# Loading the experts' second matrix with two neighbouring rows per partition

## The reference

```
hdn   = x @ w_mlp1[e] + b_mlp1[e]                      # w_mlp1[e]: 1024 x 2048
x_glu = min(hdn[:, ::2], 7)
x_lin = clip(hdn[:, 1::2], -7, 7)
act   = x_glu * sigmoid(1.702 * x_glu) * (x_lin + 1)   # tokens x 1024
y     = act @ w_mlp2[e] + b_mlp2[e]                    # w_mlp2[e]: 1024 x 1024
```

## Time and profile before

| | |
|---|---|
| median of 3 runs | 1247.48 us |
| the profiled execution | 1247.71 us |
| its span, first to last instruction | 1245.9 us |
| TensorE busy (share of the span) | 1166.1 us (94%) |
| VectorE / ScalarE busy | 407.1 / 225.8 us |
| DMA, mean over the span | 365 GB/s, 454.95 MB |
| mean granted TensorE clock | 0.997 of full speed |

### The profile page before, as it was taken

The page is one execution under the profiler, slowest core; times in us unless marked ns, Lnnn a source line. Parts: engine busy times, 40 slices in busy tenths (PEclk is TensorE's granted clock), DMA queues, the critical chain, the costliest instruction groups (busy, mean ns, idle before and its releaser), DMA issues.

```text
span 1245.9 us, 13489 instructions
## 1 busy us (share of the span) xinstructions
PE 1166.1 (94%) x5408; PEld 531.5 (43%) x5408; DVE 407.1 (33%) x674; ACT 225.8 (18%) x344; POOL 8.7 (1%) x17
## 2 busy tenths in 40 slices
PE   8999999999999999999999999899999998999997
PEld 5887777876333333333233333233333332333232
DVE  4765656764322222322222222222222222222221
ACT  3544546442001000100011000000000000000001
POOL 0100000000000000000000000000000000000000
PEclk9999999999999999999999999999999999999999
DMA  9654443689999999999999999999999999999996
GB/s 356 235 176 161 144 152 124 191 324 417 386 417 417 418 417 417 418 416 418 417 417 418 417 417 417 417 417 417 417 417 417 418 417 417 417 417 417 416 417 263
DMA packets 95908, 454.95 MB, mean 365 GB/s; under 512 B 7376, under 2 KB 7408, under 8 KB 62896
## 3 DMA queue, kind: packets, MB, share of 16 engines
q1 hardware_dynamic: 94112, 449.34, 89.7%
q10 hardware_dynamic: 960, 2.44, 0.6%
q0 software_dynamic: 784, 2.38, 0.6%
HBM read 453.09 MB, written 1.05 MB: 365 GB/s over the span
## 4 chain that ended last, share of the span: by engine, by line
PE 50%; DMA 41%; SPq 3%; DVE 3%; ACT 2%; issue 2%; ACTq 0%; DVEq 0%
PE PS L1404 13%; DMA raw<-in_w_mlp 13%; DMA merge_raw<-in_w_mlp 9%; DMA hi_raw<-in_w_mlp 9%; PE PS L1410 8%; PE PS L1234 5%; PE PS L1232 5%; PE PS L1233 4%; PE PS L1440 4%; DMA gate_raw<-in_w_mlp 4%; DMA prob_raw<-in_w_mlp 2%; DMA mT<-in_w_mlp 2%; DMA low_raw<-in_w_mlp 2%; SPq L495 2%; PE PS L1382 1%
## 5 line engine op out<-in xcount | busy, mean ns | idle before, releaser
L1404 PE MATMUL PS<-merge_raw,XG 128*64 128x512 f32 x640 | 145.9, 597 | 8.2 <-DMA merge_raw<-in_w_mlp 8.0
L1142 DVE TENSOR_SCALAR hT<-PS 128x512 f32<-128x512 f32 x32 | 22.1, 692 | 379.0 <-PE PS L1404 379.0
L759 ACT ACTIVATE hT<-hT 128x512 f32<-128x512 f32 x31 | 19.5, 631 | 567.1 <-DVE hT L1142 567.1
L1404 PE MATMUL PS<-raw,XG 128*64 128x512 f32 x464 | 106.4, 597 | 6.7 <-DMA raw<-in_w_mlp 6.4
L826 DVE TENSOR_TENSOR rest<-raw,mix_hi 128x2048 fp32r<-128x2048 f32 x38 | 87.0, 2292 | 53.4 <-ACT mix_hi L615 53.3
L1070 DVE COPY XG<-PS 128x512 f32<-128x512 f32 x32 | 22.1, 691 | 239.9 <-PE PS L1389 239.9
L1232 PE MATMUL PS<-mix_hi,hTh 128*128 128x512 f32 x224 | 89.8, 401 | 3.2 <-DVE hTl L998 1.6
L1077 DVE TENSOR_TENSOR X<-X,PS 128x512 f32<-128x512 f32 x120 | 74.4, 682 | 51.9 <-PE PS L1440 51.9
L1234 PE MATMUL PS<-mix_hi,hTl 128*128 128x512 f32 x224 | 89.4, 399 | 0.0
L1404 PEld LDWEIGHTS PS<-merge_raw,XG 128*64 128x64 f32 x640 | 43.1, 136 | 106.5 <-issue 79.1
L1233 PE MATMUL PS<-rest,hTh 128*128 128x512 f32 x224 | 88.3, 394 | 0.0
(11 more groups left out here) (276 smaller groups left out, 1221.5 us busy)
## 6 DMA issues: line engine op xcount, KB each, us to landing
merge_raw<-in_w_mlp SPq DMA_DIRECT2D x115, 1024.0 KB, 21.6
raw<-in_w_mlp SPq DMA_DIRECT2D x91, 1024.0 KB, 22.0
hi_raw<-in_w_mlp SPq DMA_DIRECT2D x65, 1024.0 KB, 21.7
gate_raw<-in_w_mlp SPq DMA_DIRECT2D x46, 1024.0 KB, 22.1
raw<-in_w_in SPq DMA_DIRECT2D x25, 1024.0 KB, 5.0
prob_raw<-in_w_mlp SPq DMA_DIRECT2D x23, 1024.0 KB, 22.3
mT<-in_w_mlp SPq DMA_DIRECT2D x22, 1024.0 KB, 21.8
low_raw<-in_w_mlp SPq DMA_DIRECT2D x21, 1024.0 KB, 22.0
```

The costliest lines, as they stand in the source:

```text
L1404: mm = pe.matmul(PS[h * SL:(h + 1) * SL, n * 512:(n + 1) * 512], XG[:, u, :], tile[:, h * D + n * 512:h * D + (n + 1) * 512], start=False, ...
```

## The change

Three things are edited. A down tile now has rows 256v + 2p and 256v + 2p + 1 on partition p, which are neighbours in memory; the halves of the last tile take every second row. The transposes of the activations take every second column, so that `AT` is grouped in the same way: chunk c reads columns 256(c // 2) + c % 2 and on, in steps of 2. At the end, the scatter of the item before stands ahead of the last item's second down tile, not its third, and ScalarE makes both of its copies before it starts its first store.

```diff
@@ -492,8 +492,7 @@
             def load_w2(e, v, tile, landed):
-                sp.dma_start(tile[:, :].rearrange("p (k n) -> p k n", k=2),
-                             w2[e, 2 * v * P:(2 * v + 2) * P, :].rearrange("e (k p) n -> p (e k) n", p=P)).then_inc(landed, 16)
+                sp.dma_start(tile[:, :], w2[e, 2 * v * P:(2 * v + 2) * P, :].rearrange("e (p k) n -> p (e k n)", k=2)).then_inc(landed, 16)
@@ -531,8 +530,8 @@
                     for c, half_in in enumerate((landed, last_half)):
-                        rows = (2 * v + c) * P
-                        sp.dma_start(tile[:, c * D:(c + 1) * D], w2[e, rows:rows + P, :].rearrange("e p n -> p (e n)")).then_inc(half_in, 16)
+                        sp.dma_start(tile[:, c * D:(c + 1) * D],
+                                     w2[e, 2 * v * P + c:(2 * v + 2) * P:2, :].rearrange("e p n -> p (e n)")).then_inc(half_in, 16)
@@ -783,6 +782,7 @@
             for t in range(TT):
                 act.wait_ge(sc_pe, 4 * (j - 1) + 2 * t + 1)
                 act.activation(X[:, t, 0:512], banks[LAST_BANK[t, 0]], ACT.Copy).then_inc(end_act, 1)
+            for t in range(TT):
                 act.wait_ge(end_act, t + 1)
                 act.dma_start(out[0, t * P:(t + 1) * P, 0:512], X[:, t, 0:512]).then_inc(out_dma, 16)
@@ -1428,7 +1428,7 @@
                 for c in range(4):
-                    mm = pe.transpose(out[:, c * P:(c + 1) * P], act_t[:, c * P:(c + 1) * P], ident)
+                    mm = pe.transpose(out[:, c * P:(c + 1) * P], act_t[:, 2 * P * (c // 2) + c % 2:2 * P * (c // 2 + 1):2], ident)
                 mm.then_inc(tr_pe, 1)
@@ -1509,7 +1509,7 @@
             for v in range(W2U):
                 tile, landed, count = last_down_tile(v)
-                if v == 2:
+                if v == 1:
                     pe.wait_ge(yc, j)
                     pe.wait_ge(st_act, j)
```

## The result

The changed kernel takes 1237.12 us, median of 4 runs (1234.83 to 1237.92), against 1246.57 us for the kernel before on the same chip (4 runs, 1245.56 to 1248.07). The ratio is 0.992, with a 95% interval of 0.9902 to 0.9938: 9.5 us less by the medians, where 8.1 were forecast, an amount that lies in the interval (7.7 to 12.2 us). The time lies 2.3 us under the forecast of 1239.4, at the lower edge of the range (1237.0 to 1243.0) and just outside the likeliest case's own (1237.5 to 1241.5). The profiled run took 1237.45 us, its span is 1235.6, before 1245.9: 10.2 us less. A second comparison of the same two kernels is among the experiments (ratio 0.9923).

The account below looks back on a forecast made before the run. The prediction took the weight stream from about 340 us as the bound. Loads -7.6, scatter -0.63 and stores +0.13 sum to -8.1 us: 1247.71 to 1239.6, less 0.23 to the runs' median, 1239.4 us; range 1237.0 to 1243.0.

Parts of the forecast that it names:

- the likeliest case: The whole kernel: the forecast of 1239.4 us itself, with its own range 1237.5 to 1241.5 and chance 0.75.
- what bounds the kernel: Whole kernel: the stream of weights sets the end from about 340 us, when it runs without a break.
- savings ahead of it are lost: Before 340 us: a microsecond saved in the stream is lost there, so only items 2 to 31 count.
- the packets as the cause: Down-tile loads: 256 packets of 4 KB against an up tile's 128 of 8 KB; one more packet costs 8 ns.
- the price of a down tile, 0.064 us: Weight stream: a down tile takes 2.553 us, an up tile 2.489; 119 tiles at 0.064 give 7.6 us.
- the transposes' weight loads: TensorE, four an item: reading every second float was taken to stay at 140 ns, costing 0.
- the second rival: TensorE: strided transposes so slow that TensorE sets the end; at ten times 140 ns, 1313 us. Chance 0.03.
- the scatter and the stores: Kernel's end: the earlier scatter saves 0.63 us; ScalarE's later first store costs 0.13 us.
- The line rate: Down-tile loads: 4 KB pieces are as good as 8 KB, w_mlp2's place makes them slow; 1247.0 us. Chance 0.10.
- The slower TensorE: Transposes: strided weight loads make TensorE set the end, from 0.63 us more for each load. Chance 0.03.
- The buffers in the first 200 us: Catching-up stage: SP's waits for buffers leave gaps, so only tiles after 537 us count; 1241.1 us. Chance 0.12.
- The two longer down legs: Stream after 537 us: two down legs 1.2 us longer, cause unknown; 2.4 us more won if packets cause it.

Follow-up runs that it names:

- the ninth experiment: The changed kernel, with the down tiles of items 0 and 1 loaded in the old pieces of 4 KB: 1237.62 us.
- The first experiment: The changed kernel, with the up tiles of all items but the last two loaded in pieces of 4 KB: 1252.2 us, ratio 1.0046 to the kernel before.
- the third: The changed kernel, with up tiles loaded as four 2 KB pieces a partition from one block without a gap (output not the reference's): 1289.67 us.
- the last: The changed kernel, with neighbouring tiles loaded in pairs of 2 MB (16 KB pieces), only from the 42nd load on: 1230.57 us, ratio 0.9867 to the kernel before.
- the wide version: The changed kernel, with 100 pairs of neighbouring tiles each loaded as one 2 MB transfer in 16 KB pieces: 1232.76 us, ratio 0.9889 to the kernel before.
- the second experiment: The changed kernel, with up tiles loaded as 2 KB pieces out of four blocks of 128 rows (output not the reference's): 1645.56 us.

## Why the prediction was right, and where it was off

**Right: what bounds the kernel.** The stream from 340 us on set the end, after the change too. Four profiles with the old down tiles have 880.5 to 880.8 us of steady stream, five with the new ones 872.0 to 872.9, and the time follows. That savings ahead of it are lost has less behind it: the ninth experiment fits, with 1237.62 us for 1,024 packets more, but could hardly have shown 0.6 us.

**Right: the packets as the cause.** It was the argument with the least behind it, since the trace before had a single stream with each kind of piece. The first experiment moved the pieces to the other matrix and the slowness went with them; the third and the last gave the same price at 2 KB and at 16 KB. The Trainium skill (DMA: Bandwidth & Descriptors, Specifications) gives 512 B as enough for line rate; these runs disagree, with 388, 410, 422 and 428 GB/s at pieces of 2, 4, 8 and 16 KB (1.049 MB over 2.705, 2.560 and 2.485 us, and 2.097 MB over 4.90). The same page (Why small descriptors are slow) states a fixed overhead of about 3 cycles for each packet, and speaks of it for small ones. These runs agree that there is one, and find it at 2 to 16 KB too, at 9.2 ns; no run here measures a cycle to set beside it.

**Off: the price of a down tile, 0.064 us.** This is the step that failed, a term of the right sum with the wrong size. The stream gained 8.26 us over its 117 down tiles (four of each of items 2 to 30, and the last item's first), 0.071 each, where the prediction took 7.6 us from 119 at 0.064. It had compared two legs of the same trace, 10.21 us for four down tiles and 19.91 for eight up tiles, and took the second as free of the first. It isn't quite. By the landings of the kernel before, the last up tile of a leg takes 2.493 us (median) where the others take 2.482 to 2.488, and the last down tile 2.535 where the others take 2.558 to 2.560: some of what the down tiles cost stands in the up leg ahead of them. With the new tiles the down leg lands in 9.94 us, not in half of 19.91, and the up leg falls too, from 19.91 to 19.88: 0.29 us less an item by these medians, where the prediction has 4 x 0.064 = 0.26. Why the cost shows one tile early stays open.

That is 0.7 of the 2.3 us. Another 0.9 is the kernel before itself, whose median was 1247.48 us in the three runs that the forecast was scaled to and is 1246.57 with the fourth; the rest is no more than the scatter of the runs (1234.83 to 1237.92). The time missed the likeliest case's own range by 0.4 us, so either of the two, put right, would have brought it in. The forecast was of the difference, and of that 8.26 + 0.50 = 8.8 us are accounted for, step by step, against 9.5 by the medians of one comparison and 9.0 by the other (1246.43 to 1237.42).

**Off, and it cost nothing: the transposes' weight loads.** 207 ns, not 140. VectorE's read of PSUM with a step, 692 ns beside 691, was the wrong neighbour for TensorE's read of SBUF: the bound from above, four plain reads, held, and the value taken did not. The sum held because it had been built not on the 140 but on TensorE's slack, and the threshold worked out for the second rival, 0.77 us a load, was far off. The Trainium skill (SBUF — State Buffer, the note on cachelines) has it that reads stay at full rate with two or more hits in a line of 16 bytes; the step of two disagrees with that here, and the step of four, with one hit in a line, costs hardly more than the step of two (210 against 207 ns).

**Right: the scatter and the stores.** 0.62 us for 0.63, and 0.09 for 0.13; together the end gave 0.50 us, as forecast. The halves of the last tile, whose rows now lie 8 KB apart, brought no wait: the three tiles run on in one group of 5.37 us.

**The rivals.** The line rate fell with the first experiment. The slower TensorE came a tenth of the way to the point from which it decides (67 ns of 630). The buffers in the first 200 us: the window from 400 to 500 us has 421 GB/s, and SP's waits for TensorE's up tiles, at down and up loads together, went from 238.5 + 124.7 to 57.7 + 185.4 us. The ring lost no time.

**The two longer down legs**, which the prediction left open, are still there, 10.90 and 10.92 us (before 11.36 and 11.41), so they don't go with the weights' packets. The traces show what they go with: loads of instructions, as told at the end.

## What to carry to other kernels

In a kernel that one steady stream of weights bounds, look at the length of the pieces even when all are far above the size that is called enough: here each packet cost its engine 9 ns, 3% of the rate from 8 KB down to 4 KB, and choosing which rows share a partition made the pieces longer at no cost in time. Count such a gain only from where the stream runs without a break, and mind that a longer transfer needs more buffers free at once, which delayed the wide version's profiled run by 4.9 us in its starved stretch. (The medians with and without that, 1232.76 and 1230.57, come from two comparisons whose ratios' intervals touch.) Measure the price of a transfer from landing to landing over the whole stream, and not as the difference of two neighbouring legs. And when an experiment goes far wrong, look which of its tiles are slow before blaming what was meant to differ.

## What the runs showed of the hardware

**Four loads in a row of the same pieces are slow.** Tiles 4 to 7 of an item in the second experiment, 2 KB pieces read again and again, landed every 5.76 us (182 GB/s), tiles 0 to 3, pieces of the same size and distance but all different, every 2.65 (395 GB/s). The mechanism is open.

**A zero-packet tile.** The line through 8, 16 and 32 packets meets none at 2.41 us a MB, an estimate from those landings, or 435 GB/s. The Trainium skill (DMA: Bandwidth & Descriptors, Specifications) gives 435 GB/s as the fabric's ceiling; the highest steady rate here is 428.

**A step in TensorE's weight load has one price.** For 128 x 128 floats 140 ns without, 207 with a step of two, 210 with four.

**Single DMA engines stall where instructions are loaded.** The page counts 43 packets of another queue, of the kind `instruction`, before and after:
```profile
q8 instruction: 43, 0.70, 0.2%
```
In the trace each is 16 KB and takes 1.0 to 1.3 us. In the kernel before 29 of them start between 350 and 1215 us, and at all 29 the sixteen increments of one tile come late, by 1.3 to 1.8 us summed over the sixteen; the changed kernel has 29 of 29 too. They come every 26 to 27 us while TensorE's items do, and every 30 us once its items follow the stream. When the engine that falls back is the one that is last anyway, the tile itself is late: such packets start at 557.8, 800.2 and 1042.8 us, and the tiles that land at 560.55, 802.89 and 1045.24 us come 3.7 to 3.8 us after the one before, in place of 2.5. The latter two close the two longer down legs, 8 items apart; the first is the wait of 1.84 us in the earlier trace rows. No run changed these packets; what the traces show is that they coincide.

**The 16 engines drift apart.** Between the first and the sixteenth increment of one tile lie 0.2 us at the first tile and 7.7 us at the 368th of the kernel before (7.5 in the changed one, 6.5 to 7.6 in eight more), and it grows at those places, as single engines fall back by about a microsecond. At the stream's end that shows as a tail, here of the kernel before (columns as in rows 5):
```profile
1226.00:1229.00 3.00, 1.94 (x8) 0.51 (x9) 0.00 (x0) 0.60 (x1) 0.00 (x0) 1.00 0.97 389
1229.00:1232.00 3.00, 2.59 (x12) 0.88 (x14) 0.00 (x0) 0.00 (x0) 0.00 (x0) 1.00 0.59 240
1232.00:1236.00 4.00, 4.00 (x18) 1.17 (x16) 0.00 (x0) 0.00 (x0) 0.00 (x0) 1.00 0.40 161
```
The engines that are ahead run out first, and the rate falls from 389 to 161 GB/s over 10 us.
